# Rounded parts and rests for the products of two attention stages over a memory

## The chip, the core and the metric

One core of a Trainium2 chip runs the whole program in one launch. TensorE (PE) multiplies matrices and loads their weights (PEld), VectorE (DVE) and ScalarE (ACT) do elementwise work, GpSimd (POOL) a few small things, and DMA queues, mostly fed by SyncE (SP), bring the weights. The metric is the device time of the launch in microseconds (us).

## The reference, cut to what matters

Two blocks of a network follow each other on 256 tokens of width 1024. The second has two cross attentions over a memory of 256 tokens, with 4 heads of 256:

```python
def mem_cross_attention(h, mem_n, w_q, w_kv, w_o):
    q = (h @ w_q).reshape(bsz, seq, MEM_HEADS, MEM_HEAD_DIM)
    k, v = jnp.split(mem_n @ w_kv, 2, axis=-1)
    ...
    s = jnp.einsum("bshd,bmhd->bhsm", q, k).astype(jnp.float32) * (MEM_HEAD_DIM ** -0.5)
    p = jax.nn.softmax(s, axis=-1).astype(v.dtype)
    o = jnp.einsum("bhsm,bmhd->bshd", p, v).reshape(bsz, seq, D_MODEL)
    return o @ w_o
```

Around them stand four feed-forward networks, a Fourier mixer with grouped attention, a short convolution and a causal attention of 8 heads of 128.

## The kernel before

All activations lie feature by token: 8 blocks of 128 features by S = 256 tokens. The weights come as tiles of 128x2048 fp32 (one tile: 1024 inputs by 256 outputs) in a fixed order, STREAM (line 38). RING is 3: three buffers `raw` and three `wt`. Each tile passes through the same steps. SP starts its transfer when the rest of the tile three before is there. ACT copies it into `wt[.., 0]` as fp32r, a rounded form of fp32 that TensorE multiplies faster (`split`, L876). DVE subtracts, `raw` minus rounded, into `wt[.., 1]` (`split`, L1212). PE multiplies with three products: rounded weight by rounded activation and by its rest in one matmul of 512 columns (L409, L480), and the weight's rest by the rounded activation in one of 256 (L441, L483).

The two memory stages are `memory_attention("mem0")` and `memory_attention("mem1")`. PARTS (lines 32 to 37) lists their weight tiles: two neighbouring heads' worth of feature blocks, `pair(i)`, of queries q, keys k or values v. mem0 has v0, q0, q1, q2, q3, v1, v2, v3 (its keys come out of the grouped attention stage), mem1 has v0, q0, q1, k2, q2, k3, q3, v1, v2, v3 (keys 0 and 1 come out of the causal stage). AHEAD = 4 tiles are multiplied before the attention loop begins. The rest are cut into pieces by rows of the contraction, PIECES (line 104): `(j, k0, k1)` is tile j over the blocks k0 to k1, and O0, O1 are the first two tiles of the output projection.

On PE, `attention` (L710) issues scores(0) and scores(1). Then for each unit n (one head, 4 in a stage) come the first pieces, four transposes of the probabilities (L739) into the PSUM bank acc[2], scores(n + 2) (L723), the second pieces, and the values (L751). Scores and values of a unit are four fp32 products of 128x128 by 128x256 each. PE takes its instructions in this order, and semaphores (`wait_ge`) hold it where an operand isn't ready.

On ACT, for each tile: `rest_part` copies the part of PSUM that holds the rest's product (L888, L892), `after(j)` rounds the weight tile j + 3. For each unit: the copy of the transposed probabilities (L1059), the exponentials (L1031), the rounding of the output (L1068). On DVE, for each tile: `part` (L1432) adds what ACT copied to the rest of PSUM and writes q_t, k_t or v_s (L1317 with L1329 for keys, L1441 for values), then `after(j)` subtracts weight tile j + 2 (L1212). For each unit: the maxima (L1521), `normalise` (L1527, L1531) and the rest of the output (L1538). Each engine takes its instructions in the order of its program: in `attention` of DVE (L1506) `rest(n - 1)`, `pieces(n, 0)`, `maxima(n + 2)`, `normalise(n + 2)`, `pieces(n, 1)`; before the loop `maxima(0)`, `maxima(1)`, `normalise(0)`, `after(...)`, `normalise(1)`.

```python
                def pieces(n, i):
                    for j in ended(kind, n, i):
                        part(kind, j)
                        ...
                            after(FIRST[kind] + j)
```

Of the kernel before, what the change touches and what calls it, by code (L numbers as in the profile page):

```python
# [6 lines left out]
F32 = mybir.dt.float32  # L7
# [6 lines left out]
P = 128  # L14
# [158 lines left out]
def program(nc, weights, x_t, mem_t, vectors, consts, fourier, fnet_w, positions, out_t):  # L173
    ctx = ExitStack()
    with ctx:
# [13 lines left out]
        h = sb("h", [P, FF, 2, S], F32R)  # L189
        q_t = sb("q_t", [P, KB, S])  # L190
# [13 lines left out]
        r_2 = sb("r_2", [P, S])  # L204
        scratch = sb("scratch", [P, 8, S])
# [17 lines left out]
        mem = k_t[:]  # L223

# [30 lines left out]
        def pair(b):  # L255
# [29 lines left out]
                             "a_rounded", "a_split"))  # L285
        z_whole, tap_begun, tap_whole, tap_scaled = (sem(n) for n in ("z_whole", "tap_begun", "tap_whole", "tap_scaled"))
# [22 lines left out]
        def plan(kind):  # L309
            units = []  # L310
            for n in range(UNITS[kind]):
                if kind == "moba":
                    units.append(dict(q=[q_t[:, n, :]], k=[k_t[:, n, :]], v=[v_s[:, :, n * P:(n + 1) * P]],
                                      rows=slice(0, P), blocks=(n, n + 1), causal=True, v_tile=MOBA.index(("v", n // 2))))
                else:
                    parts = PARTS[kind]
                    units.append(dict(q=[q_t[:, 2 * n + i, :] for i in range(2)],
                                      k=[k_t[:, 2 * n + i, :] for i in range(2)],
                                      v=[v_s[:, :, (2 * n + i) * P:(2 * n + i + 1) * P] for i in range(2)],
                                      rows=slice(0, P), blocks=(2 * n, 2 * n + 2), causal=False,  # L320
                                      qk_tile=max(parts.index(p) for p in (("q", n), ("k", n)) if p in parts),
                                      v_tile=parts.index(("v", n))))
            return units

# [81 lines left out]
        def _(pe):  # L406
# [303 lines left out]
            def attention(kind, ready):  # L710
                u0, units = UNIT0[kind], plan(kind)

                def scores(n):
                    u, a = u0 + n, units[n]
                    pe.wait_ge(a_exp, u - 1)
                    if "qk_tile" in a:
                        out_of(pe, kind, a["qk_tile"])
                    if kind == "moba":
                        pe.wait_ge(head_turned, ROPES.index(("q", n // 2)) + 1)
                    for t in range(NT):  # L720
                        keys = (t + 1) * P if a["causal"] else S
                        for i in range(len(a["q"])):
                            mm = pe.matmul(acc[u % 2][:, t, 0:keys], a["q"][i][:, t * P:(t + 1) * P],  # L723
                                           a["k"][i][:, 0:keys], start=i == 0, stop=i == len(a["q"]) - 1)
                    mm.then_inc(a_scores, 1)
# [6 lines left out]
                for n, a in enumerate(units):  # L732
# [3 lines left out]
                    pe.wait_ge(a_turned_copied, u)  # L736
                    for t in range(NT):
                        for kt in range(t + 1 if a["causal"] else NT):
                            mm = pe.transpose(acc[2][:, kt, t * P:(t + 1) * P], probs[u % 2][:, t, kt * P:(kt + 1) * P],  # L739
                                              c("ident"))  # L740
# [3 lines left out]
                    pieces(kind, n, 1, ready)  # L744
                    out_of(pe, kind, a["v_tile"])
# [119 lines left out]
        def _(act):  # L865
# [46 lines left out]

            def round_pair(b, src, gain, dst):
                for k in range(2 * b, 2 * b + 2):
                    e = act.activation(dst[:, k, 0, :], src[:, k, :], ACT.Copy, scale=v(gain, k))  # L915
                e.then_inc(rounded, 1)
# [105 lines left out]
            def attention(kind):  # L1022
# [12 lines left out]
                def pieces(n, i):  # L1035

                    for j in ended(kind, n, i):
                        rest_part(kind, j)
                        if kind != "moba" or i == 0 or j != ended(kind, n, i)[-1]:
                            after(FIRST[kind] + j)  # L1040

# [6 lines left out]
                after(FIRST[kind] + AHEAD[kind] - 1)  # L1048
                for n, a in enumerate(units):
# [8 lines left out]
                    else:  # L1058
                        act.activation(probs_t[u % 2], acc[2], ACT.Copy).then_inc(a_turned_copied, 1)  # L1059
# [97 lines left out]
            def ahead(kind):  # L1157
                for j in range(AHEAD[kind]):
                    rest_part(kind, j)
                    if j < AHEAD[kind] - 1:  # L1160
                        after(FIRST[kind] + j)

# [37 lines left out]
        def _(dve):  # L1200
# [248 lines left out]

            def query_factors(kind):  # L1450
# [55 lines left out]
            def attention(kind):  # L1506
# [34 lines left out]
                def pieces(n, i):  # L1541
                    for j in ended(kind, n, i):
# [3 lines left out]
                        if kind != "moba" or i == 0 or j != ended(kind, n, i)[-1]:  # L1546
                            after(FIRST[kind] + j)

# [8 lines left out]
                normalise(1)  # L1557
                for n in range(len(units)):
                    if n:
                        rest(n - 1)  # L1560
                    pieces(n, 0)
                    if n + 2 < len(units):
# [173 lines left out]
            def memory_attention(kind):  # L1736
# [3 lines left out]
                after(FIRST[kind])  # L1740
                factors(kind, col_x)
                after(FIRST[kind] + 1)
                query_factors(kind)
                for j in range(int(ahead), AHEAD[kind]):
                    part(kind, j)
                    if 1 < j < AHEAD[kind] - 1:
                        after(FIRST[kind] + j)
                attention(kind)
# [175 lines left out]
```

## Time and profile before

| what | value |
|---|---|
| median of 3 runs | 1246.09 us (1245.28 to 1246.23) |
| the profiled execution | 1245.89 us |
| its span, first to last instruction | 1244.1 us |
| mean granted TensorE clock | 0.999 |
| busy share of the span | PE 99%, PEld 88%, DVE 74%, ACT 53%, POOL 2% |
| instructions | 18051 |
| HBM read | 219.52 MB, 177 GB/s over the span |

The page says for each engine how long it was busy. In the timelines, a row has the start in us from the span's start, the length in us, the engine, the line, the operation, the tiles written and read with their shapes, and the number of instructions merged; in brackets stands for how long the engine had been idle before, and what ended that. A matmul's record lasts longer than its place in the queue, because the next one overlaps it; what a piece of work takes of PE is the distance from its start to the start of the next. An fp32 product shows as two records.

### The profile page before, as it was taken

The numbers are of one execution on the slowest core, as the hardware profiler recorded it, in microseconds if no ns is written. First come the engines' busy times: TensorE is split into PE (matmuls) and PEld (weight loads), VectorE is DVE, ScalarE is ACT, GpSimd is POOL, SyncE is SP. The second block draws the span as 40 slices with busy tenths as digits, with TensorE's granted clock in tenths as the row PEclk, the third lists the DMA queues.
The fourth block names the chain that finished last, engine by engine and source line by source line (L and its number), as shares of the span: only waits on it lengthen the run. The fifth ranks groups of instructions, "written<-read, shape, count | busy, mean of one in ns | idle before, by whom it ended". The sixth has DMA issues, their size and how long they took to land.

```text
span 1244.1 us, 18051 instructions
## 1 busy us (share of the span) xinstructions
PE 1233.8 (99%) x7420; PEld 1097.8 (88%) x7420; DVE 926.3 (74%) x1283; ACT 658.7 (53%) x870; POOL 31.1 (2%) x23
## 2 busy tenths in 40 slices
PE   9999999999999999999999999999999999999998
PEld 7888889878888888888888888889998888888887
DVE  7887866678877867989568777659977657877744
ACT  6665544465655544546556555445555445555632
POOL 0000000000000000440000000000000000000000
PEclk9999999999999999999999999999999999999999
DMA  9565654134555663455335555644434533555660
GB/s 322 187 214 194 226 197 163 68 131 146 198 194 178 206 234 136 170 203 204 136 135 215 192 202 174 227 176 139 167 136 174 199 135 136 203 190 183 193 214 34
DMA packets 51426, 221.74 MB, mean 178 GB/s; under 512 B 4464, under 2 KB 5776, under 8 KB 30864
## 3 DMA queue, kind: packets, MB, share of 16 engines
q1 hardware_dynamic: 51056, 220.25, 50.8%
q8 instruction: 59, 0.97, 0.3%
q10 hardware_dynamic: 288, 0.33, 0.1%
q14 instruction: 23, 0.19, 0.0%
HBM read 219.52 MB, written 1.05 MB: 177 GB/s over the span
## 4 chain that ended last, share of the span: by engine, by line
PE 90%; DVE 7%; ACT 1%; issue 1%; DMA 1%; SPq 0%; DVEq 0%; ACTq 0%
PE bank L409 47%; PE bank L441 20%; PE bank L413 7%; PE bank L430 4%; DVE wt L1212 3%; PE bank L480 2%; PE bank L723 2%; PE bank L751 2%; PE bank L457 1%; PE bank L483 1%; DVE xn L1221 1%; DVE x L1226 1%; DVE x L1227 1%; PE bank L462 1%; DMA raw<-weights 1%
## 5 line engine op out<-in xcount | busy, mean ns | idle before, releaser
L1212 DVE TENSOR_TENSOR wt<-raw,wt 128x2048 fp32r<-128x2048 f32 x202 | 464.1, 2299 | 68.0 <-ACT wt L876 67.5
L876 ACT ACTIVATE wt<-raw 128x2048 fp32r<-128x2048 f32 x202 | 386.0, 1911 | 119.4 <-PE bank L413 90.8
L409 PE MATMUL bank<-xn,wt 128*128 128x512 f32 x1712 | 415.7, 393 | 3.1 <-DVE xn L1221 2.9
L409 PEld LDWEIGHTS bank<-xn,wt 128*128 128x128 f32 x1712 | 312.8, 188 | 65.3 <-DVE xn L1221 5.3
L441 PEld LDWEIGHTS bank<-xn,wt 128*128 128x128 f32 x1856 | 238.5, 191 | 9.8 <-DVE wt L1212 0.5
L409 PE MATMUL bank<-h,wt 128*128 128x512 f32 x1004 | 246.1, 392 | 0.0
L441 PE MATMUL bank<-xn,wt 128*128 128x256 f32 x1856 | 242.5, 283 | 0.1
L409 PEld LDWEIGHTS bank<-h,wt 128*128 128x128 f32 x1004 | 182.5, 188 | 34.1 <-issue 0.4
L1317 DVE TENSOR_TENSOR scratch<-bank,rest 128x512 f32<-128x512 f32 x98 | 67.6, 689 | 86.6 <-ACT rest L888 86.5
L951 ACT ACTIVATE h<-scratch 128x256 fp32r<-128x256 f32 x88 | 36.8, 418 | 158.4 <-DVE scratch L1357 158.4
L888 ACT ACTIVATE rest<-bank 128x512 f32<-128x512 f32 x114 | 67.6, 593 | 68.3 <-PE bank L441 68.3
L413 PEld LDWEIGHTS bank<-h,wt 128*128 128x128 f32 x700 | 91.8, 191 | 4.6
L413 PE MATMUL bank<-h,wt 128*128 128x256 f32 x700 | 93.5, 282 | 0.0
L1341 DVE TENSOR_TENSOR scratch<-scratch,r_x 128x512 f32<-128x512 f32 x86 | 59.6, 693 | 2.9
L915 ACT ACTIVATE xn<-x,vec 128x256 fp32r<-128x256 f32 x62 | 28.1, 501 | 55.8 <-DVE x L1227 55.4
L441 PEld LDWEIGHTS bank<-h,wt 128*128 128x128 f32 x384 | 50.9, 191 | 2.8
L441 PE MATMUL bank<-h,wt 128*128 128x256 f32 x384 | 52.0, 282 | 0.0
L1226 DVE SCALAR_TENSOR_TENSOR x<-bank,x 128x512 f32<-128x512 f32 (+1 forms) x39 | 24.9, 637 | 30.6 <-PE bank L441 18.1
L1357 DVE TENSOR_TENSOR scratch<-scratch 128x256 f32<-128x256 f32 x88 | 36.8, 418 | 4.7 <-ACT scratch L949 4.7
L430 PE MATMUL bank<-xn,wt 128*128 128x256 f32 x288 | 39.6, 288 | 0.6 <-DVE xn L1221 0.6
L949 ACT ACTIVATE scratch<-scratch 128x256 f32<-128x256 f32 x88 | 35.8, 406 | 5.9 <-DVE scratch L1341 5.0
L430 PEld LDWEIGHTS bank<-xn,wt 128*128 128x128 f32 x288 | 36.1, 191 | 1.5 <-DVE xn L1221 1.0
(215 smaller groups left out, 963.5 us busy)
## 6 DMA issues: line engine op xcount, KB each, us to landing
raw<-weights SPq DMA_DIRECT2D x158, 1024.0 KB, 4.9
raw<-weights SPq DMA_DIRECT2D x88, 512.0 KB, 5.0
raw<-weights SPq DMA_DIRECT2D x8, 256.0 KB, 4.3
k_t<-mem_t SPq DMA_DIRECT2D x2, 1024.0 KB, 7.4
raw<-weights SPq DMA_DIRECT2D x8, 128.0 KB, 4.1
out_t<-work SPq DMA_DIRECT2D x4, 256.0 KB, 2.3
x<-x_t SPq DMA_DIRECT2D x3, 256.0 KB, 5.5
v_s<-fourier SPq DMA_DIRECT2D x2, 256.0 KB, 5.2
```

The lines of the kernel that those rows point to most:

```text
L409: return pe.matmul(out, hi, a.rearrange("p a s -> p (a s)"), start=first, stop=False, skip_group_check=True)
L413: return pe.matmul(out[:, S:2 * S], lo, a[:, 0, :], start=False, stop=last, skip_group_check=True)
L430: pe.matmul(out[:, m, 0:S], w[:, 0, m * KB + k, :], a[:, k, i, :], start=k == i == 0, stop=False, skip_group_check=True)
L441: mm = pe.matmul(home, w[:, 1, m * KB + k, :], a[:, k, 0, :], start=False, stop=k == KB - 1, skip_group_check=True)
L876: act.activation(wt[t % RING][:, 0], raw[t % RING][:], ACT.Copy).then_inc(weight_hi, 1)
L888: act.activation(rest_s[i % 3][:], src, ACT.Copy).then_inc(rest_copied, 1)
L951: act.activation(h[:, j, 0, :], gate, ACT.Copy).then_inc(h_rounded, 1)
L1212: dve.tensor_tensor(wt[t % RING][:, 1], raw[t % RING][:], wt[t % RING][:, 0].bitcast(F32), ALU.subtract).then_inc(weight_lo, 1)
L1226: link(dve.scalar_tensor_tensor(home, out[:, :, S:2 * S], scale, home, ALU.mult, ALU.add))
L1317: e = dve.tensor_tensor(dst, pair_banks(name, j)[:, :, 0:S], rest_s[i % 3][:], ALU.add)
L1341: dve.tensor_tensor(gu_s[j % 3], gu_s[j % 3], both(r_x[:]), ALU.mult).then_inc(drained, 1)
L1357: dve.tensor_tensor(gate, gate, up, ALU.mult).then_inc(whole, 1)
```

## The change

In both memory stages the queries, keys, values and transposed probabilities each become two fp32r tensors, a rounded part (`_hi`) and its rest (`_lo`), and each fp32 product becomes three fp32r products: rounded by rounded, and the two of rounded by rest. ACT writes the rounded parts of q, k, v (`part_rounded`) and, in its copy out of PSUM, of the probabilities. DVE writes the rests (`part_split`, `turned_rest`). q_lo, k_lo and v_lo take the addresses of q_t, k_t and v_s; the rounded parts lie in blocks 8 to 19 of `h`, the probabilities' rest in blocks 20 and 21. `memory_scores` and `memory_values` take the place of the fp32 products, and wait for parts_split and turned_split. The causal stage stays as it was. Empty lines are left out of the diff, and of each hunk one line of context stands before what changes.

```diff
...
         h = sb("h", [P, FF, 2, S], F32R)
+        with ExitStack() as given_back:
+            q_lo, k_lo = (given_back.enter_context(nc.sbuf_tensor(n, [P, KB, S], F32R)) for n in ("q_lo", "k_lo"))
+            v_lo = given_back.enter_context(nc.sbuf_tensor("v_lo", [P, NT, D], F32R))
...
         r_2 = sb("r_2", [P, S])
+        with nc.sbuf_tensor("turned", [P, 8, S], F32R) as turned:
+            pass
...
         mem = k_t[:]
+        spare = [h[:, a:b].rearrange("p k i s -> p (k i) s") for a, b in ((8, 12), (12, 16), (16, 20), (20, 22))]
+        q_hi, v_hi, k_hi = spare[0], spare[1].rearrange("p (t m) s -> p t (m s)", t=NT), spare[2]
+        turned_hi = [turned[:, 4 + 2 * i:6 + 2 * i, :] for i in range(2)]
+        turned_lo = [spare[3][:, 2 * i:2 * i + 2, :] for i in range(2)]
...
                              "a_rounded", "a_split"))
+        parts_rounded = {what: sem(f"{what}_rounded") for what in "qkv"}
+        parts_split = {what: sem(f"{what}_split") for what in "qkv"}
+        turned_split = sem("turned_split")
...
             return units
+        def pair_of(n):
+            return range(2 * n, 2 * n + 2)
+        def keys_beside(kind):
+            return [i for i in range(KP) if ("k", i) not in PARTS[kind]]
...
                 u0, units = UNIT0[kind], plan(kind)
+                m0 = KP * int(kind == "mem1")
+                def memory_scores(n):
+                    u = u0 + n
+                    pe.wait_ge(parts_split["q"], m0 + n + 1)
+                    pe.wait_ge(parts_split["k"], m0 + n + 1)
+                    for t in range(NT):
+                        for b in pair_of(n):
+                            for queries, keys in ((q_hi, k_hi), (q_hi, k_lo), (q_lo, k_hi)):
+                                mm = pe.matmul(acc[u % 2][:, t, :], queries[:, b, t * P:(t + 1) * P], keys[:, b, :],
+                                               start=b == 2 * n and queries is q_hi and keys is k_hi,
+                                               stop=b == 2 * n + 1 and queries is q_lo, skip_group_check=True)
+                    mm.then_inc(a_scores, 1)
+                def memory_values(n):
+                    u = u0 + n
+                    pe.wait_ge(parts_split["v"], m0 + n + 1)
+                    pe.wait_ge(turned_split, m0 + n + 1)
+                    pe.wait_ge(a_split, u)
+                    for i, b in enumerate(pair_of(n)):
+                        for kt in range(NT):
+                            for values, weights_t in ((v_hi, turned_hi), (v_lo, turned_hi), (v_hi, turned_lo)):
+                                mm = pe.matmul(acc[3][:, i, :], values[:, kt, b * P:(b + 1) * P], weights_t[u % 2][:, kt, :],
+                                               start=kt == 0 and values is v_hi and weights_t is turned_hi,
+                                               stop=kt == NT - 1 and weights_t is turned_lo, skip_group_check=True)
+                    mm.then_inc(a_out, 1)
                 def scores(n):
                     u, a = u0 + n, units[n]
                     pe.wait_ge(a_exp, u - 1)
-                    if "qk_tile" in a:
-                        out_of(pe, kind, a["qk_tile"])
                     if kind == "moba":
                         pe.wait_ge(head_turned, ROPES.index(("q", n // 2)) + 1)
+                    else:
+                        memory_scores(n)
+                        return
...
                     pe.wait_ge(a_turned_copied, u)
+                    if kind != "moba" and m0 + n:
+                        pe.wait_ge(turned_split, m0 + n)
...
                     pieces(kind, n, 1, ready)
+                    if kind != "moba":
+                        memory_values(n)
+                        continue
...
                     rest(kind, j, col_m, SPREAD_AT["mem"])
+            def part_rounded(kind, what, i):
+                if (what, i) in PARTS[kind]:
+                    out_of(act, kind, PARTS[kind].index((what, i)))
+                elif kind == "mem0":
+                    out_of(act, "gqa", i)
+                else:
+                    out_of(act, "moba", MOBA.index(("m", i)))
+                if what == "v":
+                    dst, src = (t[:, :, 2 * P * i:2 * P * (i + 1)] for t in (v_hi, v_s))
+                else:
+                    dst, src = (t[:, pair(i), :] for t in ((q_hi, q_t) if what == "q" else (k_hi, k_t)))
+                act.activation(dst, src, ACT.Copy).then_inc(parts_rounded[what], 1)
...
                             after(FIRST[kind] + j)
+                        if kind != "moba":
+                            part_rounded(kind, *PARTS[kind][j])
...
                 after(FIRST[kind] + AHEAD[kind] - 1)
+                if kind != "moba":
+                    part_rounded(kind, *PARTS[kind][AHEAD[kind] - 1])
...
                     else:
-                        act.activation(probs_t[u % 2], acc[2], ACT.Copy).then_inc(a_turned_copied, 1)
+                        act.activation(turned_hi[u % 2], acc[2], ACT.Copy).then_inc(a_turned_copied, 1)
...
                     rest_part(kind, j)
+                    for i in keys_beside(kind)[j:j + 1]:
+                        part_rounded(kind, "k", i)
                     if j < AHEAD[kind] - 1:
                         after(FIRST[kind] + j)
+                        part_rounded(kind, *PARTS[kind][j])
...
                     scaled(kind, j, k_t[:, pair(i), :], (r_m if of_memory else r_x)[:])
+            def part_split(kind, what, i):
+                done = KP * int(kind == "mem1") + i + 1
+                dve.wait_ge(parts_rounded[what], done)
+                if what == "v":
+                    dst, src, hi = (t[:, :, 2 * P * i:2 * P * (i + 1)] for t in (v_lo, v_s, v_hi))
+                else:
+                    dst, src, hi = (t[:, pair(i), :] for t in ((q_lo, q_t, q_hi) if what == "q" else (k_lo, k_t, k_hi)))
+                dve.tensor_tensor(dst, src, hi.bitcast(F32), ALU.subtract).then_inc(parts_split[what], 1)
...
                             after(FIRST[kind] + j)
+                        if kind != "moba":
+                            part_split(kind, *PARTS[kind][j])
+                def turned_rest(n):
+                    u = u0 + n
+                    dve.wait_ge(a_turned_copied, u + 1)
+                    dve.tensor_tensor(turned_lo[u % 2], acc[2], turned_hi[u % 2].bitcast(F32), ALU.subtract).then_inc(turned_split, 1)
...
                 normalise(1)
+                if kind != "moba":
+                    part_split(kind, *PARTS[kind][AHEAD[kind] - 1])
                 for n in range(len(units)):
                     if n:
                         rest(n - 1)
                     pieces(n, 0)
+                    if kind != "moba":
+                        turned_rest(n)
...
                 after(FIRST[kind])
+                for i in keys_beside(kind)[0:1]:
+                    part_split(kind, "k", i)
                 factors(kind, col_x)
                 after(FIRST[kind] + 1)
                 query_factors(kind)
+                if ahead:
+                    part_split(kind, *PARTS[kind][0])
                 for j in range(int(ahead), AHEAD[kind]):
                     part(kind, j)
+                    for i in keys_beside(kind)[j:j + 1]:
+                        part_split(kind, "k", i)
                     if 1 < j < AHEAD[kind] - 1:
                         after(FIRST[kind] + j)
+                    if j < AHEAD[kind] - 1:
+                        part_split(kind, *PARTS[kind][j])
```

## Rows read from the trace of the kernel before

**Rows 1.** first part of the page: busy us (share of the span) x instructions

```profile
PE 1233.8 (99%) x7420; PEld 1097.8 (88%) x7420; DVE 926.3 (74%) x1283; ACT 658.7 (53%) x870; POOL 31.1 (2%) x23
```

**Rows 2.** busy by window: length, PE, PEld, DVE, ACT, POOL; PEclk, DMA share, GB/s

```profile
569.84:642.00 72.16, 72.16 (x408) 63.68 (x407) 44.47 (x72) 37.03 (x55) 0.00 (x0) 1.00 0.41 146
```

**Rows 3.** timeline of PE, first memory stage: start us, us, what

```profile
598.81 0.60 PE L739 MATMUL bank<-con,scratch 128*128 128x128 f32 x4
...
606.57 1.89 PE L751 MATMUL bank<-scratch,v_s 128*128 128x256 f32 x8
...
608.30 0.60 PE L739 MATMUL bank<-con,scratch 128*128 128x128 f32 x4
...
613.26 2.00 PE L480 MATMUL bank<-wt,mn 128*128 128x512 f32 x8
...
616.05 1.89 PE L751 MATMUL bank<-scratch,v_s 128*128 128x256 f32 x8
...
621.02 2.46 PE L480 MATMUL bank<-wt,mn 128*128 128x512 f32 x10
...
624.51 1.89 PE L751 MATMUL bank<-scratch,v_s 128*128 128x256 f32 x8
...
628.34 0.60 PE L739 MATMUL bank<-con,scratch 128*128 128x128 f32 x4
...
632.96 1.89 PE L751 MATMUL bank<-scratch,v_s 128*128 128x256 f32 x8
```

**Rows 4.** chain that ended last, in order of time, the stage between

```profile
856.73 3.84 PE bank L430 x32
```

**Rows 5.** two lines: ns min/median/max; L1538 by groups: busy us, mean ns

```profile
L1153 ACT ACTIVATE h<-scratch x4: 631/632/636, 505.9 to 553.6; 128x512 fp32r<-128x512 f32 x4
...
L1732 DVE TENSOR_TENSOR h<-scratch,h x4: 710/710/712, 506.5 to 554.3; 128x512 fp32r<-128x512 f32 x4
...
L1538 DVE TENSOR_TENSOR h<-bank,h 128x512 fp32r<-128x512 f32 x4 | 2.8, 692 | 6.8 <-ACT h L1068 6.8
```

**Rows 6.** timeline of DVE, both memory stages

```profile
597.74 2.28 DVE L1212 TENSOR_TENSOR wt<-raw,wt 128x2048 fp32r<-128x2048 f32 x1
...
599.94 0.16 DVE L1527 RECIPROCAL small<-small 128x2 f32<-128x2 f32 x1
...
600.14 0.61 DVE L1531 TENSOR_SCALAR scratch<-scratch,small 128x256 f32<-128x256 f32 x2
...
615.12 2.28 DVE L1212 TENSOR_TENSOR wt<-raw,wt 128x2048 fp32r<-128x2048 f32 x1
...
631.13 2.28 DVE L1212 TENSOR_TENSOR wt<-raw,wt 128x2048 fp32r<-128x2048 f32 x1
...
988.55 2.28 DVE L1212 TENSOR_TENSOR wt<-raw,wt 128x2048 fp32r<-128x2048 f32 x1
```

**Rows 7.** timelines of DVE and PE where PE waited

```profile
656.61 0.88 DVE L1221 SCALAR_TENSOR_TENSOR xn<-x,vec,xn 128x256 fp32r<-128x256 f32 x2 [0.46 <-ACT xn L915]
...
657.54 1.20 PE L409 MATMUL bank<-xn,wt 128*128 128x512 f32 x4 [0.40 <-DVE xn L1221]
```

**Rows 8.** timeline of PE, second memory stage

```profile
987.12 1.09 PE L409 MATMUL bank<-mn,wt 128*128 128x512 f32 x4
...
988.52 0.60 PE L739 MATMUL bank<-con,scratch 128*128 128x128 f32 x4
...
988.96 1.89 PE L723 MATMUL bank<-k_t,q_t 128*128 128x256 f32 x8
...
1009.92 1.55 PE L480 MATMUL bank<-wt,mn 128*128 128x512 f32 x6
...
1012.02 1.90 PE L751 MATMUL bank<-scratch,v_s 128*128 128x256 f32 x8
```

**Rows 9.** busy time by window, the end of the program; PEclk: granted clock

```profile
1238.80:1241.00 2.20, 0.02 (x1) 0.00 (x0) 2.15 (x4) 0.00 (x0) 0.00 (x0) 1.00 0.26 97
...
1241.00:1244.10 3.10, 0.00 (x0) 0.00 (x0) 0.33 (x1) 0.00 (x0) 0.00 (x0) 0.69 0.72 270
```

## Prediction

> **What bounds the kernel now.** I read the page's busy shares first, then the busy time of each engine over the first memory stage, and last the timelines of PE, DVE and ACT inside both stages. The shares say that TensorE is busy for 99% of the span and VectorE for 74% [rows 1]. In the window of the first memory stage PE is busy 72.16 us of 72.16, at full clock; DVE is busy 44.47 (62%), ACT 37.03 (51%), DMA moves at 0.41 of its time [rows 2]. So PE, which takes its instructions in the order written, sets the end: each microsecond taken off its queue in these stages is a microsecond of the total, and each wait put into its queue is one too. There is no slack behind the stages that could take up a delay, since PE is also the bound of what follows [rows 1]. DVE and ACT have idle time on average, but an average says nothing of when a particular result is due. The question is therefore: how much shorter do the products get, and at which points does PE now arrive before the new operands are there?
>
> **Part 1, the products: -4.6 us.** A group of scores or of values in a memory stage is four fp32 products, which the trace shows as eight matmul records. From the start of values(0) to the start of the transposes behind it pass 608.30 - 606.57 = 1.73 us [rows 3], 0.43 us for each product. The new form is three fp32r products of 256 columns for each. The trace has the same shape in the stage between: 32 of them in 3.84 us, 0.12 us each [rows 4], with a weight load for each as here. A group becomes 12 x 0.12 = 1.44 us, 0.29 less. There are 4 units with two groups in each of two stages, 16 groups: 16 x 0.29 = 4.6 us. All of it lies on PE, so all of it counts. The transposes stay as they are. The bounds: no gain at all if the mix of fp32 transposes and fp32r products costs something at each change, and 4.6 if not; changes between both kinds stand in the queue before already, without a gap on PE [rows 2], so I take 4.6.
>
> **Part 2, the new work on ACT and DVE.** In each stage ACT rounds 12 pieces (four of q, k, v) and DVE subtracts 12, plus four subtractions for the turned probabilities; the rounding of those is the copy that ACT made before. The nearest rows are the same operation in the convolution stage: 0.63 us for the rounding and 0.71 for the subtraction, of 128x512 [rows 5]. Per stage that is 12 x 0.63 = 7.6 us on ACT and 16 x 0.71 = 11.4 on DVE, so DVE goes to about 56 of 72 us. Neither becomes the bound by its sum. What they cost depends on their place in the queues.
>
> **Part 3, where PE waits.** Before, scores needed q as soon as DVE had drained it, and values needed v likewise. Now they need the subtracted rest, and in DVE's program (pieces and ahead) the order for a tile j is: part, then after, then part_split. after is the subtraction for a weight tile, L1212, which holds DVE for 599.94 - 597.74 = 2.20 us [rows 6]. It stands between the drain and the split; the next queries, keys or values wait behind it and PE behind them. I count from the moment at which PE goes from the tile to its next piece:
> - a tile of v: to the start of L1212 615.12 - 613.26 = 1.86 us [rows 3, 6], then 2.20, then 0.71 for the split, and 0.05 until PE starts: 4.82 us. The 0.05 is from a wait that the trace shows, where DVE's xn ended at 656.61 + 0.88 = 657.49 and PE began at 657.54 [rows 7].
> - a tile of q: 988.55 - 987.12 = 1.43 [rows 6, 8], and the same 2.20, 0.71 and 0.05: 4.39 us. ACT is done earlier in both: its own weight rounding and the 0.63 end before DVE comes to the split.
> - the last tile of v: L1212 begins at 631.13 - 628.34 = 2.79 after it [rows 3, 6], because the copy of the turned probabilities stands before it on ACT; behind L1212 come the split (0.63 to the next start, with the 0.08 by which an instruction overlaps the next, as L1212 does: 2.28 long, 2.20 to the next start) and turned_rest (0.69, as the nearest subtraction out of PSUM [rows 5]): 2.79 + 2.20 + 0.63 + 0.69 + 0.05 = 6.36.
>
> Against that stands what PE has to do before it needs the operand. First stage: values(1) is due 616.05 - 613.26 = 2.79 after its tile, a wait of 2.03; values(2) 624.51 - 621.02 = 3.49 after, a wait of 1.33; values(3) 632.96 - 628.34 = 4.62 after, a wait of 1.74 [rows 3]. scores(3) is due 4.67 after the fourth q (half a tile, values(0), the transposes), over 4.39: no wait, with 0.3 to spare. Second stage, where more tiles stand in the loop: scores(2) is due 988.96 - 987.12 = 1.84 after its q, a wait of 2.55; scores(3) 1.44 + 0.44 = 1.88 after, a wait of 2.51; values(1) 1012.02 - 1009.92 = 2.10 after, a wait of 2.72 [rows 8]; values(2) and values(3) repeat the first stage's pattern, 2.79 and 4.62: 2.03 and 1.74.
> The ninth wait is scores(2) of the first stage. Its q tile is the last of those done ahead, and its split stands behind normalise(0), L1212 and normalise(1). These begin at 597.74 and 599.94 in the kernel before, and the multiplications at 600.14 take 0.61 - 0.08 = 0.53 to the next start [rows 6]; the seven splits ahead of the first maxima mostly fall into DVE's idle time and push this by 0.1 us by my walk of its queue. So the split runs from 600.8 to 601.5 and PE starts at 601.57. PE is through the transposes at 598.81 - 2 x 0.29 + 0.44 = 598.67 [rows 3, 8]: a wait of 2.9.
> Sum: 2.9 + 2.03 + 1.33 + 1.74 = 8.0 in the first stage, 2.55 + 2.51 + 2.72 + 2.03 + 1.74 = 11.55 in the second, 19.5 together. A run of four products after a wait takes 1.20 us where one without takes 1.09 [rows 7, 8]: nine restarts add 0.11 each, 1.0 us.
>
> **The sum.** 1245.9 (the profiled execution: 1244.1 of span and 1.8 around it; the median of the runs is 0.2 above) - 4.6 + 19.5 + 1.0 = 1261.8 us. Bounds: each wait may be 0.2 off, +-1.8 in all; the points that I have at nothing (scores(1), the first transposes and scores(3) of the first stage, each with 0.2 to 0.3 to spare) may cost up to 0.4 each; the products may give nothing (+4.6). SBUF addresses, semaphores and the unchanged copies cost nothing: q_lo, k_lo and v_lo lie where q_t, k_t and v_s lie, and the copy out of PSUM only changes its output type.
>
> **Rivals.**
> - The waits aren't there, faster: if the splits came straight behind the drains, that is if the 2.20 us of L1212 did not stand before them, the paths would be 2.62 and 2.19, under what PE has left in most places; the second stage would keep 0.35 + 0.31 + 0.52, the others nothing. Then 1245.9 - 4.6 + 1.2 + 0.3 = 1242.8. The kernel turns faster once the waits and restarts add up to less than 4.6. For it speaks DVE's idle time (38%) [rows 2], against it the written order, in which DVE can't go past L1212. 4%.
> - The waits are smaller, by half at some points, because ACT and DVE come to the tile earlier than the rows of before say: 1250 to 1257. 6%.
> - The feed of weights falls behind: DVE's queue grows by 11.4 us in each stage, the weight subtractions slip, their transfers (issued when the subtraction of three tiles before is done) slip too, and PE waits for weights also. Each such wait would be near the split's 0.7 us, for some 10 tiles in each stage up to +14, more likely half: 1262 + 6 = 1268. Against it: the pieces of a stage are the same 2.79 us for each half on PE, and DVE has 2.20 + 0.71 + 0.69 and under 1 for the drain to do in the time of a whole one. 8%.
> - The clock falls. After PE's last work at 1238.8 the granted clock was still 1.00 over the first 2.2 us without matmuls, and 0.69 on average over the 3.1 us after that [rows 9]. Four waits are 2.5 to 2.9 us long. If the clock went to its lower level (1.2 for 2.4 GHz) in each of them and stayed there for a tile's length, each would cost one more tile, 2 x 2.79 us [rows 3]: +22, 1284. 8%, since the row has the clock unchanged for nearly so long. The Trainium skill, TensorE: Matmul & The Clock Gate, section "Why this matters for your kernels", warns of this: a pause between bursts of matmuls can bring the halved clock back. By that rule longer waits are worse than their own length; the trace's row agrees that a longer pause lowers the clock, and shows none that was followed by work.
>
> **How the numbers follow.** The forecast has 74% (1258 to 1266), the clock 8%, the feed 8%, smaller waits 6%, none 4%. The range from 1256.5 to 1268 holds the forecast, about half of the feed's cases and a part of the smaller waits, 8 in 10. What can be told from no change is about 0.2%, 2.5 us. Slower by more: all but the last case and a remainder, 95%; faster 4%, within it 1%.
>
> **What would show it.** In the profile after, PE's waits should show three in the first stage for values (about 2.0, 1.3, 1.7) and one for scores (2.9), and five in the second, each released by DVE's subtraction (part_split, the last of each stage by turned_rest), with L1212 right before the split on DVE; a group of 12 products should take 1.44 us; outside the two stages nothing should move but by the shift, 16 us at the end: some 6.1 us after the first stage and 9.8 more after the second. It is wrong if PE's queue shows waits under 1 us there (the order on DVE isn't what I read), if waits are put down to ACT's rounding or to weights, or if the granted clock in the windows of the stages is under 1.

## The result and the profile after

The changed kernel takes 1267.95 us (median of 4 runs, 1265.84 to 1268.39), the kernel before beside it 1245.86. The ratio is 1.0174, with a 95% interval from 1.0162 to 1.0187: slower by 22 us. The forecast was 1261.8, in a range from 1256.5 to 1268.0. So the sign and most of the size are right, the time lies 0.05 us inside the upper edge of the range, and 6 us are missing from the sum.

The profiled execution has a span of 1265.8 us. Of its page, the busy shares, which answer to [rows 1], and the line of the granted clock:

```profile
PE 1237.1 (98%) x7484; PEld 1102.3 (87%) x7484; DVE 945.8 (75%) x1315; ACT 670.9 (53%) x894; POOL 31.1 (2%) x23
...
PEclk9999999999999999999999999999999989999999
```

PE is busy 3.3 us longer than before although its products became shorter, and idle for 28.7 us in place of 10.3. The clock, 9 tenths or more in every slice before, has one slice at 8. The list of waits on PE says who ended the new idle time ("issue" where the profile names no releaser):

```profile
PE bank L757 <- DVE v_lo L1534: 10.6, 6, 2.5
PE bank L744 <- issue: 7.4, 3, 2.5
PE bank L431 <- DVE xn L1297: 2.9, 6, 0.9
```

L744 is the new scores, three waits, L757 the new values, six: nine in all. Only the third row is older, and it was 2.9 us before, too. The timeline of PE in the first stage, in the places of [rows 3], in pairs of the piece before a wait and the first product after it:

```profile
598.33 0.60 PE L791 MATMUL bank<-con,scratch 128*128 128x128 f32 x4
601.47 0.36 PE L744 MATMUL bank<-h 128*128 128x256 f32 x1 [2.54 <-issue]
...
608.55 0.29 PE L757 MATMUL bank<-turned,h 128*128 128x256 f32 x1
...
609.98 0.60 PE L791 MATMUL bank<-con,scratch 128*128 128x128 f32 x4
610.33 0.36 PE L744 MATMUL bank<-h 128*128 128x256 f32 x1
...
616.48 1.11 PE L505 MATMUL bank<-wt,mn 128*128 128x256 f32 x8
619.44 0.39 PE L757 MATMUL bank<-turned,h 128*128 128x256 f32 x1 [1.85 <-DVE v_lo L1534]
...
628.09 1.35 PE L505 MATMUL bank<-wt,mn 128*128 128x256 f32 x10
630.60 0.38 PE L757 MATMUL bank<-turned,h 128*128 128x256 f32 x1 [1.16 <-DVE v_lo L1534]
...
637.41 1.59 PE L463 MATMUL bank<-h,wt 128*128 128x256 f32 x12
640.60 0.35 PE L757 MATMUL bank<-turned,h 128*128 128x256 f32 x1 [1.59 <-DVE v_lo L1534]
...
649.07 3.82 PE L431 MATMUL bank<-h,wt 128*128 128x512 f32 x16
```

A group of 12 products takes 609.98 - 608.55 = 1.43 us (1.44 forecast, 1.73 before), and four transposes before an fp32r product 0.35 in place of 0.44. The waits, from the end of the earlier piece's place in the queue: 598.33 + 0.36 to 601.47 is 2.78; 616.48 + 8 x 0.119 to 619.44 is 2.01; 628.09 + 10 x 0.119 to 630.60 is 1.32; 637.41 + 12 x 0.119 to 640.60 is 1.76. In the second stage, which answers to [rows 8]:

```profile
995.34 0.60 PE L791 MATMUL bank<-con,scratch 128*128 128x128 f32 x4
998.35 0.35 PE L744 MATMUL bank<-h 128*128 128x256 f32 x1 [2.42 <-issue]
...
1012.59 0.60 PE L791 MATMUL bank<-con,scratch 128*128 128x128 f32 x4
1015.59 0.35 PE L744 MATMUL bank<-h 128*128 128x256 f32 x1 [2.40 <-issue]
...
1025.60 0.87 PE L505 MATMUL bank<-wt,mn 128*128 128x256 f32 x6
1029.02 0.39 PE L757 MATMUL bank<-turned,h 128*128 128x256 f32 x1 [2.55 <-DVE v_lo L1534]
...
1037.89 1.11 PE L505 MATMUL bank<-wt,mn 128*128 128x256 f32 x8
1040.86 0.38 PE L757 MATMUL bank<-turned,h 128*128 128x256 f32 x1 [1.85 <-DVE v_lo L1534]
...
1060.05 3.82 PE L431 MATMUL bank<-h,wt 128*128 128x512 f32 x16
```

These are 2.65, 2.64, 2.71 and 2.02 us, and values(3) repeats the first stage's with 1.75; 11.8 in all, and 7.9 in the first stage: 19.6 against the 19.5 of the forecast. One of the chains, that of v1 in the first stage, in the timelines of ACT and DVE (it answers to the row at 615.12 in [rows 6]):

```profile
614.84 0.84 ACT L947 ACTIVATE rest<-bank,col_m 128x256 f32<-128x256 f32 x2 [0.67 <-PE bank L505]
615.57 1.91 ACT L931 ACTIVATE wt<-raw 128x2048 fp32r<-128x2048 f32 x1
617.37 0.62 ACT L980 ACTIVATE h<-v_s 128x512 fp32r<-128x512 f32 x1
...
615.71 0.88 DVE L1517 SCALAR_TENSOR_TENSOR v_s<-bank,col_m,rest 128x256 f32<-128x256 f32 x2 [0.69 <-ACT rest L947]
616.51 2.28 DVE L1288 TENSOR_TENSOR wt<-raw,wt 128x2048 fp32r<-128x2048 f32 x1
618.71 0.68 DVE L1534 TENSOR_TENSOR v_lo<-v_s,h 128x512 fp32r<-128x512 f32 x1
```

DVE drains the tile (L1517), is held by the weight tile for 2.20 us (L1288), and only then subtracts v (L1534, 618.71 + 0.68 = 619.39); PE starts at 619.44. ACT's rounding (L980) had been done at 617.99. For the scores, where the list names no releaser, DVE's queue fits as well: q_lo's subtraction ends at 601.36 and PE starts at 601.47. For values(3) the list names v_lo, but that had been done at 639.89; it is `turned_rest` that ends at 640.49, before PE starts at 640.60.

So the waits are as forecast, and the rest of the loss is elsewhere. Of the kernel before, the stretch from the first v tile of the first stage to the third tile of its output goes from 569.84 to 641.67, after from 569.93 to 649.07: 7.3 us more where 6.1 were forecast. In the second stage the shift goes from 7.4 to 1060.05 - 1038.31 = 21.7: 14.3 more where 9.8 were forecast. Busy time by window shows what those stretches have in common; the number behind POOL's is the granted clock:

```profile
619.00:623.00 4.00, 3.56 (x18) 3.46 (x19) 1.05 (x2) 1.04 (x2) 0.00 (x0) 0.67 0.75 262
999.00:1003.00 4.00, 4.00 (x16) 3.45 (x15) 1.09 (x4) 1.20 (x4) 0.00 (x0) 0.57 0.60 242
1040.00:1044.00 4.00, 3.14 (x19) 2.85 (x20) 1.49 (x3) 0.60 (x1) 0.00 (x0) 1.00 0.65 231
```

After four of the nine waits the clock is at its lower level for part of the window (a mean of 0.56 to 0.67 in the windows behind 619, 999, 1016 and 1029.5, two of which stand here; 0.5 would be that level alone), after that at 1040.86 it is not, and neither after the first, at 601.47. The fall doesn't come at once here, and by windows of 0.2 us the lower level lasts from 620.4 to 623.8: single products after the wait at 619.44, with the start in the first column:

```profile
620.27 0.33 PE L757 MATMUL bank<-turned,h 128*128 128x256 f32 x1
620.40 0.42 PE L757 MATMUL bank<-turned,v_lo 128*128 128x256 f32 x1
620.61 0.42 PE L757 MATMUL bank<-h 128*128 128x256 f32 x1
```

The products follow each other by 0.12 us and, from 620.40 on, by 0.21. The group takes 2.03 us in place of 1.43, the transposes 0.70 in place of 0.36, the eight products of 512 columns behind them 2.67 in place of 1.84: 1.8 us lost. The same reckoning gives 1.6, 1.6 and 1.75 for the other three, 6.8 together, of which 0.3 are the restarts; without a fall a group after a wait takes 1.50 (601.47 to 602.97), 0.07 more than the others. The account closes: 16 groups x 0.295 = -4.7, shorter transposes before scores -0.4, waits +19.6, nine restarts +0.6, the clock +6.5, in all +21.6; the spans differ by 1265.8 - 1244.1 = 21.7.

### The profile page after: what moved, and what is told of

It reads as the page before. It is cut to its first block, busy times and chain, and to the rows that moved or that the text cites. A ratio compares the mean times of both kernels' runs of the same rounds, so it can differ in the third digit from the quotient of the medians.

```text
span 1265.8 us, 18237 instructions
## 1 busy us (share of the span) xinstructions
PE 1237.1 (98%) x7484; PEld 1102.3 (87%) x7484; DVE 945.8 (75%) x1315; ACT 670.9 (53%) x894; POOL 31.1 (2%) x23
## 4 chain that ended last, share of the span: by engine, by line
PE 87%; DVE 9%; issue 2%; ACT 1%; DMA 1%; SPq 0%; DVEq 0%; ACTq 0%
PE bank L431 46%; PE bank L463 20%; PE bank L435 7%; PE bank L452 4%; DVE wt L1288 4%; PE bank L502 2%; PE bank L479 1%; PE bank L757 1%; DVE xn L1297 1%; PE bank L744 1%; PE bank L505 1%; DVE x L1302 1%; DVE x L1303 1%; PE bank L484 1%; PE bank L791 1%
## 5 line engine op out<-in xcount | busy, mean ns | idle before, releaser
L1288 DVE TENSOR_TENSOR wt<-raw,wt 128x2048 fp32r<-128x2048 f32 x202 | 464.1, 2299 | 67.9 <-ACT wt L931 67.4
```

The source lines that it names most:

```text
L1288: dve.tensor_tensor(wt[t % RING][:, 1], raw[t % RING][:], wt[t % RING][:, 0].bitcast(F32), ALU.subtract).then_inc(weight_lo, 1)
```

## The experiments

The theory after the result: (a) the products gain 5 us; (b) the waits come from the place of part_split and part_rounded behind the weight tile's steps in the queues, and not from the amount of new work; (c) the remainder is the clock, which falls after some of the waits. Rivals: the products cost instead of gaining; the load on DVE is what hurts; the clock only reflects idle time. The first four experiments ran on one chip, the other three on another, each beside the kernel before.

**The products alone.** 

```diff
+        q_lo, k_lo, v_lo, turned_lo = q_hi, k_hi, v_hi, turned_hi
...
-                    pe.wait_ge(parts_split["q"], m0 + n + 1)
-                    pe.wait_ge(parts_split["k"], m0 + n + 1)
+                    if "qk_tile" in units[n]:
+                        out_of(pe, kind, units[n]["qk_tile"])
...
             def part_split(kind, what, i):
+                return
```

(likewise for the values, part_rounded and turned_rest)

> The changed kernel without the rounding and subtracting of q, k, v and without the subtraction of the turned probabilities; the three products of fp32r read old contents of h in place of the parts, so the attention's result is left out. PE waits only for what it waited for before the change. Theory (the products save 0.29 us for each of 16 groups, and waits of about 19.6 us and a lower clock take it back): 4.7 us under the kernel before, about 1241.2, perhaps 0.5 less since the transposes are followed more quickly by an fp32r product (0.36 in place of 0.44 us); no waits on PE in the stages, clock as before. Rival (three fp32r products with their 12 weight loads cost more in the queue than they save, and the waits are only a part of the loss): at or above 1246.

Measured: 1240.42 us, beside 1245.78 for the kernel before; ratio 0.9958 (0.9943 to 0.9973). That is 5.4 us less, and PE has no gap in the first stage's window:

```profile
569.84:642.00 72.16, 72.16 (x451) 65.03 (x450) 47.02 (x73) 39.63 (x57) 0.00 (x0) 1.00 0.41 144
```

So part (a) holds: three fp32r products of 256 columns with their weight loads are cheaper than one fp32 product, by what the queue's spacing said and a little more.

**The work alone.**

```diff
+                    if "qk_tile" in a:
+                        out_of(pe, kind, a["qk_tile"])
...
-                    else:
-                        memory_scores(n)
-                        return
...
-                dve.tensor_tensor(dst, src, hi.bitcast(F32), ALU.subtract).then_inc(parts_split[what], 1)
+                dve.tensor_tensor(work[:, at:at + 2, :], src, hi.bitcast(F32), ALU.subtract).then_inc(parts_split[what], 1)
```

> The fp32 products of the kernel before, with all the new roundings on ACT and all the new subtractions on DVE in their places in the two queues; the subtractions write to places that nobody reads, and no product waits for them. Theory (the work is harmless, the dependency costs): within 1.5 us of the kernel before, no wait over 0.5 us on PE in the stages. Rival (DVE's 11.4 us more in each stage delay the weight subtractions, the maxima or the probabilities until PE waits): several us slower, with PE waiting for weights or for probabilities; if all of the loss is load, about 1270.

Measured: 1245.70 us beside 1245.78, ratio 1.0000 (0.9991 to 1.0009). The same window:

```profile
569.84:642.00 72.16, 72.16 (x407) 63.68 (x406) 53.65 (x88) 43.09 (x66) 0.00 (x0) 1.00 0.41 145
```

DVE has 9.2 us more to do than in [rows 2] in that window, ACT 6.1, and PE still works for the whole of it. The load is free; the rival that it delays weights or probabilities falls.

**The waits filled.**

```diff
+                def fill(out, count):
+                    for _ in range(count):
+                        pe.matmul(out[:, 0, 0:P], ones[:], ones[:], start=True, stop=True)
...
+                    fill(acc[u % 2], {("mem0", 2): 8, ("mem1", 2): 8, ("mem1", 3): 8}.get((kind, n), 0))
                     pe.wait_ge(parts_split["q"], m0 + n + 1)
...
+                    fill(acc[3], {("mem0", 1): 5, ("mem0", 2): 3, ("mem0", 3): 5, ("mem1", 1): 8, ("mem1", 2): 5, ("mem1", 3): 5}.get((kind, n), 0))
                     pe.wait_ge(parts_split["v"], m0 + n + 1)
```

(for the values, the wait for `a_split` now stands ahead of the filling, since the matmuls of ones overwrite the bank that it guards)

> The changed kernel, with matmuls of ones by ones (fp32, 128 columns, about 0.235 us each) ahead of each of the nine waits, into the PSUM bank that the group overwrites next: 8 before the waits over 2.5 us, 5 before those of 1.7 to 2.1, 3 before the one of 1.3. They fit into the waits, so the operands come no later; PE idles 0.6 to 1 us in place of 1.3 to 2.8. Theory (about 6.5 us of the loss are stretches at the lower clock level that follow the waits): 1261.5 to 1262.5, granted clock 0.999. Rival (what is missing to the forecast are longer waits or slower products, and the clock only shows idle time): unchanged, about 1268, or slower by what the added matmuls take.

Measured: 1260.95 us (1260.81 to 1261.15) beside 1245.78, ratio 1.0123 (1.0108 to 1.0138); the mean granted clock is 1.0. More work on PE made the kernel 7 us faster than the changed one on the same chip. The timeline at scores(2), values(1) and values(3) of the first stage, and the window:

```profile
600.95 0.39 PE L749 MATMUL bank<-h 128*128 128x256 f32 x1 [0.72 <-DVE q_lo L1540]
...
616.94 1.28 PE L738 MATMUL bank<-ones 128*128 128x128 f32 x10
618.96 0.38 PE L763 MATMUL bank<-turned,h 128*128 128x256 f32 x1 [0.73 <-DVE v_lo L1540]
...
638.54 0.35 PE L763 MATMUL bank<-turned,h 128*128 128x256 f32 x1 [0.53 <-DVE h L1646]
...
592.00:650.00 58.00, 55.54 (x363) 50.26 (x363) 35.40 (x53) 27.63 (x47) 0.00 (x0) 1.00 0.32 109
```

PE reaches the group of values(1) at 616.94 and gets its operand at 618.96, 2.02 us later, as without the filling; the idle part of it is 0.73. What went is the stretch at the lower clock. Without it the kernel takes 1260.95, 0.85 under the forecast's sum of 1261.8, which had no term for the clock, and a little under what was expected here. This shows part (c). With the shorter idle times the profile also names the releasers that it left open above: q_lo's subtraction for scores(2), and `turned_rest` (L1646) for values(3).

**The changed kernel again.** Its edit is none.

> The changed kernel once more, on the same chip as the three others: about 1268, granted clock 0.993 to 0.996. By the clock theory its times go in steps of about 1.7 us with the number of waits that the clock falls after, and spread more than those of the kernel before; by the rival they spread as little as those.

Measured: 1268.02 us (1267.50 to 1268.56), clock 0.993. The spread of these four is 1.1 us and that of the kernel before 0.7, so the times don't show the expected steps; in the first set the four went from 1265.84, with a clock of 0.996, to 1268.39, with 0.993. The traces show the extra fall: the clock falls at five waits here and at four in the earlier execution, and the span is 1.0 us longer (1266.8 for 1265.8) although PE gets the operand of the first wait 0.47 us earlier (601.00 for 601.47). The trace shows, too, that the fall isn't bound to a particular wait. In this execution there is one at the first wait, where the earlier one had none:

```profile
601.00 0.55 PE L744 MATMUL bank<-h 128*128 128x256 f32 x1 [2.54 <-issue]
601.35 0.42 PE L744 MATMUL bank<-k_lo,h 128*128 128x256 f32 x1
...
600.00:600.70 0.70, 0.00 (x0) 0.00 (x0) 0.70 (x3) 0.41 (x1) 0.00 (x0) 1.00 0.57 94
600.70:601.00 0.30, 0.01 (x1) 0.04 (x1) 0.30 (x2) 0.00 (x0) 0.00 (x0) 0.50 0.00 0
601.00:605.00 4.00, 4.00 (x17) 3.77 (x18) 1.35 (x3) 0.15 (x1) 0.00 (x0) 0.61 0.63 246
```

The wait before 601.00 has the same 2.54 us of idle time as the one before 601.47 above. The granted clock is at its lower level from 600.7 on, 0.3 us before PE starts again, so here it fell within the pause.

**DVE's order changed.**

```diff
                     for j in ended(kind, n, i):
                         part(kind, j)
+                        if kind != "moba":
+                            part_split(kind, *PARTS[kind][j])
                         ...
                             after(FIRST[kind] + j)
-                        if kind != "moba":
-                            part_split(kind, *PARTS[kind][j])
...
+                    if kind != "moba" and n:
+                        turned_rest(n)
                     pieces(n, 0)
-                    if kind != "moba":
+                    if kind != "moba" and not n:
                         turned_rest(n)
```

> The changed kernel with two moves in DVE's program for the pieces of the loop: part_split before after (so before the weight tile's subtraction of 2.20 us), and for units 1 to 3 turned_rest before the first pieces. ACT keeps its order, with the weight rounding of 1.80 us before part_rounded. Theory (PE waits for the last link of a chain; with DVE's 2.20 gone ACT's 1.80 is next): a v tile's path goes from 4.82 to 0.20 + 0.73 + 1.80 + 0.63 + 0.03 + 0.71 + 0.05 = 4.15, a q tile's to 3.91, the last v tile's to 5.05. The waits become 2.8, 1.4, 0.7, 0.4 in the first stage and 2.15, 2.15, 2.0, 1.35, 0.4 in the second, 13.4 in place of 19.6: 1261.8 with the clock's losses as before, down to 1255.5 without them. Rival (the waits come from DVE's order alone): they go nearly wholly, 1245 or less.

Measured: 1257.60 us (1256.69 to 1262.52) beside 1245.81, ratio 1.0107 (1.0086 to 1.0129). Three of the waits, with the idle time in brackets (it is 0.16 to 0.24 shorter than the distance in the queue, since a matmul's record outlasts its place):

```profile
618.99 0.38 PE L757 MATMUL bank<-turned,h 128*128 128x256 f32 x1 [1.27 <-DVE v_lo L1534]
636.61 0.38 PE L757 MATMUL bank<-turned,h 128*128 128x256 f32 x1 [0.27 <-DVE v_lo L1534]
...
993.93 0.36 PE L744 MATMUL bank<-h 128*128 128x256 f32 x1 [1.94 <-issue]
```

Expected were 1.4, 0.4 and 2.15; the distances are 1.43, 0.43 and 2.17, and those of all nine waits add up to 13.5, with 13.4 expected. Taking 2.20 us off DVE's side of the chain shortened eight of the waits by only 0.5 to 1.3 each, because ACT's 1.80 us for the weight tile was next. The first stays at 2.8, as expected, since its tile is done ahead of the loop. The rival (only DVE's order) falls. The wide spread of the times fits a clock that falls in some executions and not in others; the profiled one has 0.998, with a single fall, at the wait of 2.16 us that ends at 1009.12.

**Both orders changed.**

```diff
                         rest_part(kind, j)
+                        if kind != "moba":
+                            part_rounded(kind, *PARTS[kind][j])
                         ...
                             after(FIRST[kind] + j)
-                        if kind != "moba":
-                            part_rounded(kind, *PARTS[kind][j])
```

(and the last tile done ahead: rounded before `exponentials(0)`, subtracted right after `normalise(0)`)

> As dve_split_first, and on ACT part_rounded before after in the loop; the last tile done ahead is rounded before the first exponentials and subtracted right after the first normalisation. Theory: a v tile's path is 0.20 + 0.87 + 0.83 for the drain, 0.03 + 0.63 for ACT's rounding, 0.03 + 0.71 and 0.05: 3.40 us; a q tile's 2.97. Waits of 0.6 in the first stage (values(1)) and 1.2, 1.2, 1.3, 0.6 in the second, 4.9 in all; 1245.8 - 5.4 + 4.9 + 0.4 for restarts = 1245.7, no stretch at the lower clock. Rival (what the change loses is its load on DVE and ACT): no better than dve_split_first.

Measured: 1246.29 us (1246.02 to 1246.84) beside 1245.81, ratio 1.0005 (0.9995 to 1.0014). The chain of q3 in the second stage, in a timeline of all engines:

```profile
999.20 0.60 ACT L943 ACTIVATE rest<-bank 128x512 f32<-128x512 f32 x1 [1.04 <-PE bank L463]
...
999.83 0.69 DVE L1393 TENSOR_TENSOR q_t<-bank,rest 128x512 f32<-128x512 f32 x1 [0.55 <-ACT rest L943]
...
1000.55 0.63 ACT L980 ACTIVATE h<-q_t 128x512 fp32r<-128x512 f32 x1 [0.76 <-DVE q_t L1393]
...
1001.22 0.69 DVE L1534 TENSOR_TENSOR q_lo<-q_t,h 128x512 fp32r<-128x512 f32 x1 [0.70 <-ACT h L980]
...
1002.01 0.36 PE L744 MATMUL bank<-h 128*128 128x256 f32 x1 [0.99 <-issue]
```

The chain is now the four steps of the parts alone: PSUM's rest copied, the sum, the rounding, the subtraction; 1002.01 - 999.00 = 3.01 us from PE's handover, 2.97 expected. It is still longer than the 1.8 us that PE has to do there, and the remaining waits (idle times of 0.56, 1.00, 0.99, 1.14 and 0.44 us, 5.1 us as distances in the queue) eat the whole gain of the products. The same work and the same products as in the changed kernel, in another order: 1268.0 - 1246.3 = 21.7 us less. Of these 14.5 are waits (19.6 down to 5.1), and most of the rest is the clock, which doesn't fall here. This shows part (b) for 14.5 of the 19.6 us of waits; the other 5.1 come from the length of the four steps themselves, whatever stands between them.

**A mixture.**

```diff
+        TRIPLED = {"q": [("mem0", n) for n in range(4)] + [("mem1", 0), ("mem1", 1)],
+                   "v": [("mem0", 0), ("mem0", 2), ("mem0", 3), ("mem1", 0), ("mem1", 3)]}
...
-                    else:
+                    elif tripled(kind, "q", n):
                         memory_scores(n)
                         return
+                    else:
+                        out_of(pe, kind, a["qk_tile"])
```

> As both_split_first, but the groups whose operands come late there stay fp32 products (values(1) of the first stage, scores(2), scores(3), values(1) and values(2) of the second), with neither rounding nor subtraction for them; 11 of 16 groups have three fp32r products. Theory: waits under 0.3 us in all, and 11/16 of the 5.4 us that the products alone gave, 1245.8 - 3.7 + 0.3 = 1242.4, faster than both kernels. Rival (waits come up elsewhere, since the moved steps on ACT and DVE delay exponentials, probabilities or weights): 1244 or more.

Measured: 1242.58 us (1242.06 to 1242.75) beside 1245.81, ratio 0.9972 (0.9962 to 0.9982). The windows from the first scores of each stage:

```profile
592.00:655.00 63.00, 62.59 (x391) 56.31 (x390) 46.49 (x69) 36.32 (x58) 0.00 (x0) 1.00 0.44 151
980.00:1060.00 80.00, 79.59 (x465) 70.51 (x464) 55.52 (x77) 42.35 (x57) 0.00 (x0) 1.00 0.42 148
```

The 0.41 us of idle time in each are a wait of the stages' end that the kernel before has too. It is 3.2 us faster than the kernel before, the only one of the complete kernels here that is, by having three products only where the parts are ready when PE comes.

## Why the prediction was right, and where it wasn't

- Part 1, the products: right, somewhat small. 4.6 us were forecast, the group's 0.29 is exact; the shorter transposes before scores (0.35 for 0.44) were not in it, and the products alone gave 5.4.
- Part 2, that the new work costs nothing by its amount: right, shown by the work alone.
- Part 3, the nine waits and their lengths: right to 0.15 us for each, 19.6 for 19.5 in all, and the three points with 0.2 to 0.3 us to spare indeed cost nothing. The rounding took 0.62 and the subtraction 0.68 (0.63 and 0.71 forecast). The place of the weight tile's steps in the queues was shown as the cause of most of it by moving the splits ahead of them: 13.5 us of waits with DVE's order changed, 5.1 with both. The releasers are as forecast, DVE's subtractions and, for values(3), `turned_rest`; the filled waits name them. The rival in which the waits aren't there (1242.8) left out that ACT's rounding can only begin when DVE has drained the tile: with both orders changed the path is 3.0 us for a q tile, not 2.19, and the time 1246.3.
- The restarts: 0.07 us each in place of 0.11.
- The clock: wrong, and this is the missing 6 us. The step that failed is the one in the rivals: from the row in which the clock stays at 1.00 for the first 2.2 us of idle time at the program's end [rows 9] it took the clock as nearly safe for four waits of 2.5 to 2.9 us, which are longer than that, gave the case 8% and put nothing of it into the sum. The row shows when the clock fell in one long pause, and it isn't a limit for shorter ones: here the clock fell at a wait of 2.01 us, when PE had been at work again for 0.9 us, and in the same execution not at one of 2.78; in the repeated execution it fell within that wait of 2.78. The rival's price was off the other way: a fall cost 1.6 to 1.8 us and not a tile's 5.6, so four falls were 6.5 us and not 22. One of the prediction's own signs of being wrong came true, a granted clock under 1 in the stages (0.56 to 0.67 in four windows of about 4 us). By TensorE: Matmul & The Clock Gate of the Trainium skill, section "Why this matters for your kernels", a pause between bursts lets the clock halve if it is long enough; the trace agrees in the direction, but waits of 2.01 to 2.78 us are shorter than the pauses that the page warns of, and here the measurement decides. The filled waits show that work in the pause prevents the fall.
- The range: that it holds 1267.95, by 0.05 us, is luck. Its upper part was there for a weight feed that falls behind, which didn't happen, and the clock's case stood outside it, at 1284.
- The weight feed: no wait for weights came up, as the work alone shows.

## What to carry to other kernels

When a bound engine is given operands that two others must first prepare, read the preparing steps in the order of their queues: the cost is the length of that chain, weight tiles and all, less what the bound engine has to do in the meantime, and it can be worked out before the change is made (here to 0.15 us for each of nine waits). Put the short step that somebody waits for ahead of the long one that nobody waits for yet, on every engine of the chain; moving it on one only brings the next to light. Where the chain still doesn't fit, keep the old form at those places, and count with it that waits of 2 us and more on TensorE may each cost another 1.7 us of lower clock (here ten of sixteen such waits, in three traces).

## What the runs showed of the hardware

Matmuls of ones put into the waits, which delay nothing and whose results nobody reads, made the kernel 7.1 us faster (1268.02 to 1260.95), with the idle part of each wait down to between 0.5 and 0.8 us by the timeline. Whether the clock falls at a wait of 2.0 to 2.8 us was different from one execution to the next at the same wait; what decides it was not settled here. In the traces of the changed kernel, of its repetition and of the one with DVE's order changed it fell at ten of sixteen such waits, and at none of their eleven shorter ones, of at most 1.76 us. In the two executions of the changed kernel the fall at scores(2) of the first stage was absent once and once began 0.3 us before PE started again (600.7, PE at 601.00); at values(1) of the same stage it came when PE had been at work again for 0.9 us (620.4, PE from 619.44). At the lower level products of 256 columns followed each other by 0.21 us in place of 0.12.
